# Turning the experts' gather round: one-hot blocks as weights, token rows as the moving operand

## The chip, the cores and the metric

The kernel runs on one core of a Trainium2 chip. The metric is the time of one execution in device microseconds, as the median of several runs; one more execution is taken by the profiler, and its trace is what is read below. Only TensorE (PE), VectorE (DVE), ScalarE (ACT), GpSimd (POOL) and SyncE (SP, which issues the transfers) of that core are in play.

## What is computed

One layer of a decoder over 288 tokens: 256 of one prompt and 8 sequences of 4. A mixer of two linear-attention branches, then a mixture of experts, each under a modulated norm. Everything is fp32. The part that matters here, cut from the reference (M = 288 tokens, D = 1024, 16 experts of hidden width 512, two experts for each token):

```python
def _moe(h, w_gr, b_gr, w_er, b_er, w_g, w_u, w_d):
    ...
    comb = (one_hot(group) * g_w)[:, :, None] * within[:, None, :]   # token x group x expert, two non-zero
    out = jnp.zeros_like(hf)
    for g in range(N_GROUPS):
        a = jnp.einsum('md,edf->mef', hf, w_g[g])
        u = jnp.einsum('md,edf->mef', hf, w_u[g])
        hid = jax.nn.silu(a) * u * comb[:, g, :, None]
        out = out + jnp.einsum('mef,efd->md', hid, w_d[g])
```

The kernel does not compute every expert for every token. It gathers, for each expert, up to 64 of the tokens that chose it, runs the expert on these, and scatters the results back.

## The kernel before, in words

The mixer, the output projection and the router take the first 640 us or so. The router leaves `h2t`, the 288 normed token rows in three tiles of 128, 128 and 32 tokens (`TILES`), each row of 1024 numbers; `rank`, for each token and expert its place among that expert's tokens; and `comb`, its weight.

The 16 experts are then worked off as 8 pairs, `expert_block(i)`, in the order in which they are numbered. A pair has 128 slots (`PAIR`), 64 (`SLOTS`) for each of its two experts. VectorE builds from `rank` the one-hot blocks `Dg` (token x slot, one block for each token tile) and, times `comb`, `Dc`. TensorE's order in a pair is written out by hand, and so is that of the other engines:

- gate: `hg`, the gathered rows turned (1024 features over 8 blocks of 128 partitions, 128 slots), times the gate weights into bank 2; each expert's 64 slots are one product of 64 weight columns and 512 moving columns, two of them side by side (`products`);
- three transposes of `Dc` into bank 4, from which VectorE copies the scatter matrix `DT_`;
- up: the same with the up weights into bank 3;
- `gather(i + 1)`: the next pair's rows, in both turned and gathered form in one step: for each of 8 feature blocks and each of 3 token tiles a product with 128 features of `h2t` as weights and the 128 columns of `Dg` as the moving operand, into banks 0 and 1. VectorE copies bank 0 into the first half of `hg`, ScalarE bank 1 into the second (`gather_read`, L1827 and L2229);
- four transposes of `hid`, the activated hidden rows, into bank 5, and a wait for VectorE's copy of them (L1847);
- down: 16 products into banks 6 and 7, copied by VectorE (L1850) and ScalarE (L2245) into `yt`;
- scatter: 8 products of 288 columns, into banks 4 to 7, which VectorE adds to `acc` (L1854). From the fifth on a product waits until VectorE has added the one that stood in its bank.

A pair's gate waits for both copies of `gather_read`. The first gather, `gather(0)`, stands before the loop; the last pair has none behind it. SyncE issues the transfers: each expert's weights are 3 x 2 MB, loaded for a pair at a time, 4 MB a transfer; gate weights have two buffers, up and down weights one each. The load of a pair's up weights is issued when the pair before has finished its up products, the down weights likewise, and the gate weights when the gate products two pairs before are over. Tokens beyond an expert's first 64 are handled in a loop of `overflow` blocks, which runs no block with these inputs. The norm and the output follow.

All of TensorE's instructions are recorded by two helpers, `mm` (L431) and `tr` (L434), so a line alone doesn't tell one product from another; shapes and the order do. In the records an fp32 product is two loads of weights and two streams; a transpose is one of each.

Of the kernel before, what the change touches and what calls it, by code (L numbers as in the profile page):

```python
# [19 lines left out]
ACT = mybir.ActivationFunctionType  # L20
# [132 lines left out]
def _program(nc, ctx, I, O, known):  # L153
# [130 lines left out]
    EW = carve(3, 2, 4096, at=mixer_only)  # L284
    yrow = carve(3, D, at=mixer_only)
    top[0] = persistent
    h2t = carve(3, D)
# [171 lines left out]
    def named(prefix, names):  # L459
        return {n: ctx.enter_context(nc.semaphore(f"{prefix}_{n}")) for n in names}  # L460


    STEPS = ("one_hot", "dispatch", "scatter_matrix", "scatter_matrix_read", "gathered", "gather_read0",
             "gather_read1", "gate",
             "up", "softplus_step", "softplus", "log_sigmoid", "sigmoid", "silu", "hidden", "turned", "turned_read",
# [22 lines left out]
    def _(pe):  # L488
# [504 lines left out]
        def gather(i, n):  # L993

            pe.wait_ge(n["dispatch"], i + 1)
            for g in range(2):
                for k in range(4):
                    for m, (o, w) in enumerate(TILES):
                        last = mm(pm[g][:, PAIR * k:PAIR * k + PAIR],
                                  h2t[0:w, m, 512 * g + 128 * k:512 * g + 128 * k + 128],  # L1000
                                  Dg[0:w, m].rearrange("p a b -> p (a b)"), m == 0, m == 2)
                last.then_inc(n["gathered"], 1)

        def expert_block(i, n, loaded_sem, second, gates, gates_loaded, more):
# [34 lines left out]
            for g in range(2):  # L1039
                for k in range(4):  # L1040
                    last = products(pm[6 + g], hidT, 2, k, g, 4)
                last.then_inc(n["down"], 1)
            pe.wait_ge(n["down_read0"], i + 1)
            for d in range(KD):
# [8 lines left out]
        def experts():  # L1053
# [6 lines left out]
            pe.wait_ge(*when("read h2t21"))  # L1060
            gather(0, main_sems)
            with pe.Fori(0, TWO_PAIRS) as i:
                expert_block(2 * i, main_sems, expert_loaded, 1, EW[:, 0], (expert_loaded[0], 16 * (i + 1)), True)
                expert_block(2 * i + 1, main_sems, expert_loaded, 1, gate2, (gate2_loaded, 16 * (i + 1)), True)
# [6 lines left out]
            def one_over(j):  # L1071
                gather(j, over_sems)
                expert_block(j, over_sems, over_loaded, 0, EW[:, 0], (over_loaded[0], 16 * (j + 1)), False)

# [21 lines left out]
    def _(dve):  # L1096
# [723 lines left out]
        def dispatch_pair(pair):  # L1820

            two = bass.ds(2 * pair, 2)
            dispatch(rank[:, :, two], comb[:, :, two], main_sems, pair + 1, 2)

        def gather_read(i, n):
            dve.wait_ge(n["gathered"], 2 * i + 1)
            V.tensor_copy(hg[:, 0:4, :], pm[0][:, 0:4 * PAIR].rearrange("p (k s) -> p k s", s=PAIR)) \  # L1827
                .then_inc(n["gather_read0"], 1)

        def expert_block(i, n, next_dispatch):  # L1830
# [13 lines left out]
            if next_dispatch:  # L1844
                gather_read(i + 1, n)
            dve.wait_ge(n["turned"], i + 1)
            V.tensor_copy(hidT, pm[5][:, 0:4 * PAIR].rearrange("p (k s) -> p k s", s=PAIR)) \  # L1847
                .then_inc(n["turned_read"], 1)
            dve.wait_ge(n["down"], 2 * i + 1)
            V.tensor_copy(yt[0:PAIR, 0:512], pm[6][0:PAIR, :]).then_inc(n["down_read0"], 1)  # L1850
            dve.wait_ge(n["added"], KD * i + 1)
            for d in range(KD):
# [3 lines left out]
        def experts():  # L1856
# [20 lines left out]
            step(V.tensor_copy(expB, b[:, 0:OVER]))  # L1877
            step(V.tensor_copy(rankO, mid(b[:, 16:16 + OVER], 3)), "read table", "tables")
            gather_read(0, main_sems)
            with dve.Fori(0, NE // 2 - 1) as i:  # L1880
# [4 lines left out]
            def one_over(j):  # L1885
# [13 lines left out]
                dve.wait_ge(over_sems["picked"], 6 * j + 6)  # L1899
                dispatch(rankJ.unsqueeze(2), combJ.unsqueeze(2), over_sems, j + 1, 1)  # L1900
                gather_read(j, over_sems)
                expert_block(j, over_sems, None)
# [27 lines left out]
    def _(act):  # L1930
# [275 lines left out]
        def router():  # L2206
# [16 lines left out]
            act.wait_ge(*when("ed"))  # L2223
            A.activation(rs_["p1"], rs_["p1"], ACT.Exp).then_inc(mark("router_by_scalar", "eexp"), 1)
            token_major(2)

        def gather_read(i, n):
            act.wait_ge(n["gathered"], 2 * i + 2)
            A.activation(hg[:, 4:8, :], pm[1][:, 0:4 * PAIR].rearrange("p (k s) -> p k s", s=PAIR), ACT.Copy) \  # L2229
                .then_inc(n["gather_read1"], 1)  # L2230

        def expert_block(i, n, more):
# [9 lines left out]
            if more:  # L2242
                gather_read(i + 1, n)
            act.wait_ge(n["down"], 2 * i + 2)
            A.activation(yt[0:PAIR, 512:1024], pm[7][0:PAIR, :], ACT.Copy).then_inc(n["down_read1"], 1)  # L2245

        def experts():
            gather_read(0, main_sems)
            with act.Fori(0, NE // 2 - 1) as i:
                expert_block(i, main_sems, True)  # L2250
            expert_block(NE // 2 - 1, main_sems, False)
            act.wait_ge(*when("tables"))

            def one_over(j):
                gather_read(j, over_sems)
                expert_block(j, over_sems, False)

            overflow(act, one_over)
# [18 lines left out]
    def _(pool):  # L2277
# [48 lines left out]
        def router():  # L2326
# [6 lines left out]
            G.memset(comb, 0.0)  # L2333
            G.memset(rt, 0.0).then_inc(mark("cleared", "rt zero"), 1)

            G.memset(acc, 0.0).then_inc(main_sems["added"], 1)
# [186 lines left out]
```

## Time and profile before

| what | value |
|---|---|
| time, median of 3 runs | 963.03 us (962.93 to 964.56) |
| profiled execution, its own time | 962.34 us |
| span of the profiled execution | 960.4 us |
| TensorE busy | 876.6 us (91%) |
| weight loads (PEld) busy | 594.3 us (62%) |
| VectorE busy | 399.9 us (42%) |
| ScalarE busy | 258.2 us (27%) |
| moved by DMA | 190.65 MB, mean 199 GB/s |
| transfers of expert weights | 24, of 4096 KB each |

A busy TensorE is not one at its peak: products are pipelined, and a record counts as busy while it lasts, also where the weight loads are what sets the pace. The granted clock, beside each stretch in the views by windows, is a share of the full 2.4 GHz: 1.00 is that, 0.50 is 1.2 GHz. The share of the DMA engines is a mean over 16 and can come out a little above 1.

### The profile page before, as it was taken

To read this page: it belongs to the slowest core of one execution; us is meant where nothing else is said; L and a number is where in the kernel's file an instruction comes from. 1 tells how busy PE (TensorE), PEld (TensorE's weight loads), DVE (VectorE), ACT (ScalarE), POOL (GpSimd) and SP (SyncE) were. 2 spreads that over 40 slices of the span, in tenths; PEclk is the share of its full clock that TensorE was granted. 3 is DMA by queue.
4 is the path that set the end of the run, shared out by engine and by line. 5 is a ranking of instruction groups with operands and counts; after the bars stand their busy time and mean duration, and the time that the engine had idled before them with its cause. 6 is when DMAs were issued, how large, how long until landed. Compare 5 with 4: busy or idle time off the path is not lost.

```text
span 960.4 us, 12485 instructions
## 1 busy us (share of the span) xinstructions
PE 876.6 (91%) x4791; PEld 594.3 (62%) x4791; DVE 399.9 (42%) x992; ACT 258.2 (27%) x626; POOL 35.2 (4%) x84
## 2 busy tenths in 40 slices
PE   5889999898898899999999978779999999999995
PEld 3557777666666798879887736555544544544533
DVE  3120004656687855664555384341222222222216
ACT  3121103665554333434335320121011011011012
POOL 0000000000400000000001003000000000000000
PEclk9969999999998999999999957957999999999998
DMA  8947666522557321222216318991999998997621
GB/s 206 347 142 228 205 222 213 177 89 88 172 179 240 113 87 45 88 88 69 65 44 170 108 48 246 326 387 50 349 375 338 347 377 331 354 363 265 254 96 51
DMA packets 134412, 190.65 MB, mean 199 GB/s; under 512 B 6656, under 2 KB 90283, under 8 KB 134309
## 3 DMA queue, kind: packets, MB, share of 16 engines
q1 hardware_dynamic: 134360, 189.94, 58.7%
q8 instruction: 35, 0.57, 0.2%
q14 instruction: 17, 0.14, 0.1%
HBM read 178.98 MB, written 10.95 MB: 198 GB/s over the span
## 4 chain that ended last, share of the span: by engine, by line
PE 80%; DVE 10%; ACT 4%; issue 2%; SPq 2%; DMA 1%; DVEq 0%; POOL 0%; ACTq 0%; POOLq 0%
PE bank L431 78%; PE bank L434 3%; DVE arena L1693 2%; DMA arena<-in_w_ada 1%; DVE arena L1271 1%; DVE arena L1847 1%; DVE arena L1134 1%; ACT arena L1945 1%; SPq L2365 0%; ACT arena L1938 0%; DVE arena L1256 0%; ACT arena L1936 0%; ACT arena L1949 0%; DVE arena L1571 0%; ACT arena L2042 0%
## 5 line engine op out<-in xcount | busy, mean ns | idle before, releaser
L431 PE MATMUL bank<-arena 128*128 128x288 f32 (+8 forms) x4494 | 834.9, 414 | 60.4 <-DVE arena L1158 8.6
L431 PEld LDWEIGHTS bank<-arena 128*128 128x128 f32 (+4 forms) x4494 | 559.0, 174 | 322.2 <-issue 178.2
L434 PE MATMUL bank<-arena 128*128 128x128 f32 (+6 forms) x297 | 50.3, 302 | 18.7 <-DMA arena<-in_w_conv 7.3
L434 PEld LDWEIGHTS bank<-arena 128*128 128x128 f32 (+6 forms) x297 | 35.8, 154 | 38.9 <-issue 19.5
L2042 ACT ACTIVATE arena<-arena 128x288 f32<-128x288 f32 (+1 forms) x56 | 25.1, 448 | 122.0 <-DVE arena L1256 122.0
L1854 DVE TENSOR_TENSOR arena<-arena,bank 128x288 f32<-128x288 f32 x64 | 28.8, 455 | 29.4 <-PE bank L431 28.0
L1271 DVE SCALAR_TENSOR_TENSOR arena<-arena 128x312 f32<-128x312 f32 x72 | 39.4, 547 | 2.5
L1834 DVE SCALAR_TENSOR_TENSOR arena<-bank,arena 128x512 f32<-128x512 f32 x8 | 5.5, 692 | 77.2 <-ACT arena L2239 77.2
L1125 DVE TENSOR_TENSOR arena<-bank,arena 128x18 f32<-128x18 f32 x24 | 4.2, 174 | 77.9 <-PE bank L431 77.9
L2229 ACT ACTIVATE arena<-bank 128x512 f32<-128x512 f32 x8 | 4.8, 598 | 111.7 <-PE bank L431 111.7
L1940 ACT ACTIVATE arena<-arena 128x288 f32<-128x288 f32 (+4 forms) x60 | 33.5, 558 | 2.0
L2075 ACT ACTIVATE arena<-bank 128x288 f32<-128x288 f32 x40 | 16.2, 405 | 53.9 <-PE bank L431 30.2
L1256 DVE SCALAR_TENSOR_TENSOR arena<-arena 128x288 f32<-128x288 f32 (+1 forms) x56 | 25.9, 463 | 8.7 <-ACT arena L1940 8.7
L1434 DVE TENSOR_TENSOR arena<-arena 128x512 f32<-128x512 f32 x28 | 18.9, 690 | 23.0 <-PE bank L431 23.0
L1938 ACT ACTIVATE arena<-arena 128x288 f32<-128x288 f32 (+4 forms) x60 | 28.0, 466 | 1.9
L1504 DVE TENSOR_TENSOR arena<-arena,bank 128x512 f32<-128x512 f32 x24 | 16.5, 689 | 26.6 <-PE bank L431 26.6
L1936 ACT ACTIVATE arena<-arena 128x288 f32<-128x288 f32 (+2 forms) x57 | 25.5, 448 | 4.9 <-DMA arena<-in_cc 4.1
L2235 ACT ACTIVATE arena<-bank 128x512 f32<-128x512 f32 x8 | 4.8, 597 | 81.1 <-PE bank L431 81.1
L2245 ACT ACTIVATE arena<-bank 128x512 f32<-128x512 f32 x8 | 4.8, 598 | 71.0 <-PE bank L431 71.0
L1945 ACT ACTIVATE arena<-bank,arena 128x288 f32<-128x288 f32 x19 | 9.5, 500 | 48.7 <-PE bank L431 48.7
L1850 DVE COPY arena<-bank 128x512 f32<-128x512 f32 x8 | 5.5, 691 | 32.4 <-PE bank L431 32.4
L1827 DVE COPY arena<-bank 128x512 f32<-128x512 f32 x8 | 5.5, 692 | 31.1 <-PE bank L431 31.1
(238 smaller groups left out, 441.4 us busy)
## 6 DMA issues: line engine op xcount, KB each, us to landing
arena<-in_w_in SPq DMA_DIRECT2D x36, 1024.0 KB, 6.8
arena<-in_w_exp_gate SPq DMA_DIRECT2D x8, 4096.0 KB, 13.9
arena<-in_w_exp_up SPq DMA_DIRECT2D x8, 4096.0 KB, 17.1
arena<-in_w_exp_down SPq DMA_DIRECT2D x8, 4096.0 KB, 13.0
arena<-in_w_ada SPq DMA_DIRECT2D x24, 1024.0 KB, 5.6
arena<-in_state_gla SPq DMA_DIRECT2D x4, 1024.0 KB, 6.9
out_gla_s<-arena SPq DMA_DIRECT2D x4, 1024.0 KB, 8.9
arena<-in_w_out SPq DMA_DIRECT2D x4, 1024.0 KB, 6.1
```

The costliest lines, as they stand in the source:

```text
L431: return T.matmul(out, lhsT, rhs, start=start, stop=stop)
L434: return T.transpose(out, in_, ident[0:n, 0:n])
L1256: V.scalar_tensor_tensor(sg, y, 0.0, sg, ALU.min, ALU.subtract) \
L1271: V.scalar_tensor_tensor(y, x[:, j:j + YW], wv(j), y, ALU.mult, ALU.add) \
L1434: V.tensor_tensor(Lm[0:n, hs, 0:n], LT[0:n, hs, 0:n], mid(const(f"level{lv}")[0:n, 0:n], HG), ALU.mult) \
L1693: last = V.scalar_tensor_tensor(st, st, eSs[:, s, h:h + 1], pm[4 + j][:, P * q:P * q + P], ALU.mult, ALU.add)
L1854: V.tensor_tensor(acc[:, d, :], acc[:, d, :], pm[4 + d % 4][:, 0:TOK], ALU.add).then_inc(n["added"], 1)
L1936: A.activation(dst, src, ACT.Abs).then_inc(mark(kind, event + " abs"), 1)
L1938: A.activation(dst, dst, ACT.Exp, scale=-1.0).then_inc(mark(kind, event + " exp"), 1)
L1940: A.activation(dst, dst, ACT.Ln, bias=one[0:n]).then_inc(mark(kind, event), 1)
L1945: A.activation(dst, src, ACT.Ln, bias=const("eps")[0:n], scale=scale) \
L2042: A.activation(sg, sg, ACT.Exp).then_inc(mark("proj_by_scalar", f"sig{s3}"), 1)
```

## The change

The gather makes rows first and turns them afterwards. For each half of the 1024 features there are three products, one for each token tile, with the one-hot block `Dg` (128 tokens x 128 slots) as weights and 512 columns of the token rows `h2t` as the moving operand; they give 128 slots x 512 features in bank 0 or 1. VectorE (bank 0) and ScalarE (bank 1) copy these into a new tile `rows` (`rows_read`, in the places of the old `gather_read`). A new step on TensorE, `turn_rows`, turns `rows` by eight transposes of 128 x 128 back into banks 0 and 1, and `gather_read` copies them into `hg` as before, now after the copies out of the down products. In a pair `turn_rows` for the next one stands between down and scatter; for the first pair it stands right behind `gather(0)`.

The third token tile is used at all of its 128 rows, so it is cleared once by GpSimd, ahead of the memset of `acc`, and ScalarE's copy of the third token tile waits for that. The one-hot block has zeros in the rows that no token fills.

```diff
+    rows = carve(D, at=mixer_only + 3 * 2 * 4096)
...
             for g in range(2):
+                for m in range(3):
+                    last = mm(pm[g][0:PAIR, :], Dg[:, m].rearrange("p a b -> p (a b)"),
+                              h2t[:, m, 512 * g:512 * g + 512], m == 0, m == 2)
+                last.then_inc(n["gathered"], 1)
+
+        def turn_rows(i, n):
+
+            for g in range(2):
+                pe.wait_ge(n[f"rows_read{g}"], i + 1)
                 for k in range(4):
-                    for m, (o, w) in enumerate(TILES):
-                        last = mm(pm[g][:, PAIR * k:PAIR * k + PAIR],
-                                  h2t[0:w, m, 512 * g + 128 * k:512 * g + 128 * k + 128],
-                                  Dg[0:w, m].rearrange("p a b -> p (a b)"), m == 0, m == 2)
-                last.then_inc(n["gathered"], 1)
+                    c = 4 * g + k
+                    last = tr(pm[g][:, PAIR * k:PAIR * k + PAIR], rows[0:PAIR, 128 * c:128 * c + 128], PAIR)
+                last.then_inc(n["rows_turned"], 1)
...
                 last.then_inc(n["down"], 1)
+            if more:
+                turn_rows(i + 1, n)
             pe.wait_ge(n["down_read0"], i + 1)
...
             gather(0, main_sems)
+            turn_rows(0, main_sems)
...
+        def rows_read(i, n):
+            dve.wait_ge(n["gathered"], 2 * i + 1)
+            V.tensor_copy(rows[0:PAIR, 0:512], pm[0][0:PAIR, :]).then_inc(n["rows_read0"], 1)
+
         def gather_read(i, n):
-            dve.wait_ge(n["gathered"], 2 * i + 1)
+            dve.wait_ge(n["rows_turned"], 2 * i + 1)
...
             if next_dispatch:
-                gather_read(i + 1, n)
+                rows_read(i + 1, n)
             dve.wait_ge(n["turned"], i + 1)
...
             V.tensor_copy(yt[0:PAIR, 0:512], pm[6][0:PAIR, :]).then_inc(n["down_read0"], 1)
+            if next_dispatch:
+                gather_read(i + 1, n)
             dve.wait_ge(n["added"], KD * i + 1)
...
+            act.wait_ge(*when("h2t padding"))
             token_major(2)
 
+        def rows_read(i, n):
+            act.wait_ge(n["gathered"], 2 * i + 2)
+            A.activation(rows[0:PAIR, 512:D], pm[1][0:PAIR, :], ACT.Copy).then_inc(n["rows_read1"], 1)
...
             if more:
-                gather_read(i + 1, n)
+                rows_read(i + 1, n)
             act.wait_ge(n["down"], 2 * i + 2)
             A.activation(yt[0:PAIR, 512:1024], pm[7][0:PAIR, :], ACT.Copy).then_inc(n["down_read1"], 1)
+            if more:
+                gather_read(i + 1, n)
...
+            G.memset(h2t[:, 2, :], 0.0).then_inc(mark("cleared", "h2t padding"), 1)
 
             G.memset(acc, 0.0).then_inc(main_sems["added"], 1)
```

## Rows read from the trace of the kernel before

**Rows 1.** The page: the chain that ended last, shares of the span by engine

```profile
PE 80%; DVE 10%; ACT 4%; issue 2%; SPq 2%; DMA 1%; DVEq 0%; POOL 0%; ACTq 0%; POOLq 0%
```

**Rows 2.** The chain in order of time, a period: start us, us, what

```profile
...
720.26 18.20 PE bank L431 x80
...
739.00 15.47 PE bank L431 x80
...
755.94 18.18 PE bank L431 x80
```

**Rows 3.** Windows of one period: stretch, length, busy (count), clock, DMA share, GB/s

```profile
731.35:767.02 35.67, 34.79 (x168) 17.22 (x167) 9.13 (x18) 3.78 (x6) 0.00 (x0) 1.00 0.95 353
```

**Rows 4.** Timeline: start, us, engine, line, operation, count [idle before <-releaser]

```profile
723.95 0.69 DVE L1850 COPY arena<-bank 128x512 f32<-128x512 f32 x1 [3.84 <-PE bank L431]
...
727.27 3.69 PEld L431 LDWEIGHTS bank<-arena 128*128 128x128 f32 x16 [0.81 <-issue]
727.38 0.60 ACT L2245 ACTIVATE arena<-bank 128x512 f32<-128x512 f32 x1 [7.96 <-PE bank L431]
728.13 3.78 DVE L1854 TENSOR_TENSOR arena<-arena,bank 128x288 f32<-128x288 f32 x8 [3.49 <-PE bank L431]
731.35 0.20 PEld L431 LDWEIGHTS bank<-arena 128*64 128x64 f32 x4 [0.39 <-issue]
...
745.96 8.32 PEld L431 LDWEIGHTS bank<-arena 128*128 128x128 f32 x48 [0.81 <-issue]
...
754.40 0.42 PEld L434 LDWEIGHTS bank<-arena 128*128 128x128 f32 x4
754.40 0.66 PE L434 MATMUL bank<-arena 128*128 128x128 f32 x4
```

**Rows 5.** Timeline of weight loads in the mixer, under full-width products of 512 columns

```profile
419.83 0.19 PEld L431 LDWEIGHTS bank<-arena 128*128 128x128 f32 x1 [0.24 <-issue]
420.26 0.19 PEld L431 LDWEIGHTS bank<-arena 128*128 128x128 f32 x1 [0.24 <-issue]
```

**Rows 6.** Timeline of weight loads from the first gather to the first up products

```profile
645.86 0.93 PEld L431 LDWEIGHTS bank<-arena 128*128 128x128 f32 x4 [0.22 <-issue]
...
647.73 0.93 PEld L431 LDWEIGHTS bank<-arena 128*128 128x128 f32 x4 [0.23 <-issue]
...
658.97 0.29 PEld L431 LDWEIGHTS bank<-arena 128*64 128x64 f32 x4 [0.23 <-issue]
...
659.88 0.24 PEld L431 LDWEIGHTS bank<-arena 128*64 128x64 f32 x2 [0.62 <-issue]
...
667.57 0.20 PEld L431 LDWEIGHTS bank<-arena 128*64 128x64 f32 x4
```

**Rows 7.** Where the clock rises: windows (columns of rows 3), timeline, and chain

```profile
656.00:657.00 1.00, 1.00 (x5) 0.65 (x3) 0.00 (x0) 0.00 (x0) 0.00 (x0) 0.50 0.00 0
...
661.00:662.00 1.00, 1.00 (x6) 0.28 (x4) 0.00 (x0) 0.00 (x0) 0.00 (x0) 0.95 0.00 0
...
927.00:928.00 1.00, 1.00 (x4) 0.21 (x2) 0.00 (x0) 0.00 (x0) 0.00 (x0) 0.67 0.00 0
...
930.00:931.00 1.00, 1.00 (x4) 0.28 (x3) 0.00 (x0) 0.00 (x0) 0.00 (x0) 0.63 0.00 0
...
926.80 12.86 PE L431 MATMUL bank<-arena 128*64 128x512 f32 x48 [0.88 <-DVE arena L1847]
...
579.95 38.39 PE bank L431 x144
...
586.00:588.00 2.00, 2.00 (x10) 1.38 (x9) 0.69 (x3) 0.00 (x0) 0.36 (x1) 1.00 0.94 281
```

**Rows 8.** Timeline of GpSimd: the memset of `acc`

```profile
614.79 2.02 POOL L2336 MEMSET arena<- 128x2304 f32 x1
```

**Rows 9.** Issue of one load of up weights, and its landing by the page

```profile
746.21 0.37 SPq L2431 DMA_DIRECT2D arena<-in_w_exp_up  x1
...
arena<-in_w_exp_up SPq DMA_DIRECT2D x8, 4096.0 KB, 17.1
```

More of the change, by code:

```diff
@@ L460, in named @@
         return {n: ctx.enter_context(nc.semaphore(f"{prefix}_{n}")) for n in names}
-    STEPS = ("one_hot", "dispatch", "scatter_matrix", "scatter_matrix_read", "gathered", "gather_read0",
-             "gather_read1", "gate",
+    STEPS = ("one_hot", "dispatch", "scatter_matrix", "scatter_matrix_read", "gathered", "rows_read0", "rows_read1", "rows_turned",
+             "gather_read0", "gather_read1", "gate",
              "up", "softplus_step", "softplus", "log_sigmoid", "sigmoid", "silu", "hidden", "turned", "turned_read",
@@ L1072, in one_over @@
                 gather(j, over_sems)
+                turn_rows(j, over_sems)
                 expert_block(j, over_sems, over_loaded, 0, EW[:, 0], (over_loaded[0], 16 * (j + 1)), False)
@@ L1878, in experts @@
             step(V.tensor_copy(rankO, mid(b[:, 16:16 + OVER], 3)), "read table", "tables")
+            rows_read(0, main_sems)
             gather_read(0, main_sems)
@@ L1900, in one_over @@
                 dispatch(rankJ.unsqueeze(2), combJ.unsqueeze(2), over_sems, j + 1, 1)
+                rows_read(j, over_sems)
                 gather_read(j, over_sems)
@@ L2224, in router @@
             A.activation(rs_["p1"], rs_["p1"], ACT.Exp).then_inc(mark("router_by_scalar", "eexp"), 1)
+            act.wait_ge(*when("h2t padding"))
             token_major(2)
+        def rows_read(i, n):
+            act.wait_ge(n["gathered"], 2 * i + 2)
+            A.activation(rows[0:PAIR, 512:D], pm[1][0:PAIR, :], ACT.Copy).then_inc(n["rows_read1"], 1)
         def gather_read(i, n):
-            act.wait_ge(n["gathered"], 2 * i + 2)
+            act.wait_ge(n["rows_turned"], 2 * i + 2)
             A.activation(hg[:, 4:8, :], pm[1][:, 0:4 * PAIR].rearrange("p (k s) -> p k s", s=PAIR), ACT.Copy) \
@@ L2242, in expert_block @@
             if more:
-                gather_read(i + 1, n)
+                rows_read(i + 1, n)
             act.wait_ge(n["down"], 2 * i + 2)
             A.activation(yt[0:PAIR, 512:1024], pm[7][0:PAIR, :], ACT.Copy).then_inc(n["down_read1"], 1)
+            if more:
+                gather_read(i + 1, n)
         def experts():
+            rows_read(0, main_sems)
             gather_read(0, main_sems)
@@ L2254, in one_over @@
             def one_over(j):
+                rows_read(j, over_sems)
                 gather_read(j, over_sems)
```

## The prediction

> **What bounds the kernel now.** The chain that ended last comes first: four fifths of it is TensorE work, and hardly any is a wait for a transfer [rows 1]. The same chain in order of time shows where the change sits. From 661 to 917 us it repeats with a period of 35.68 us, one period for each pair of experts, and all of it is TensorE but for one VectorE copy (L1847) [rows 2]. So a microsecond taken from TensorE inside this period is a microsecond of the end, as long as nothing else is nearly as long. One thing is: the DMA engines are 0.95 busy in a period, while VectorE and ScalarE are busy for 9.1 and 3.8 of 35.67 us [rows 3]. The timeline of one period then gives the order on TensorE: gate, three transposes, up, gather, four transposes of the hidden rows, a wait, down, scatter [rows 2, 4].
>
> In the gather the weight loads are the bound. 48 loads of 128x128 fill 8.32 us without a gap, 173 ns each [rows 4]; a product of 128 fp32 columns is made of two such load-and-stream records and streams for less than that.
>
> **Gathers 1 to 7, inside the period.** Old: from the first gather load at 745.96 to the first load of the hidden rows' transposes at 754.40, 8.44 us [rows 4]. New: per half of the 1024 columns three products (one per token tile) of a 128x128 one-hot block with 512 token columns, six products, at two records each twelve records. The trace has this very form, full width and 512 columns, at full clock: loads of 0.19 us start every 0.43 us, each hidden by the stream before it [rows 5]. So 0.2 us for the first load and 12 x 0.43 = 5.16 us. The transposes' first load can hide under the last stream, so the saving is 8.44 + 0.1 - 5.36 = 3.2 us, or 3.1 if it doesn't hide; I take 3.15. The third token tile at 128 rows instead of 32 costs columns nothing: the number of streamed columns is what it was (24 x 128 = 6 x 512).
>
> Added on TensorE: eight transposes of 128x128 between down and scatter. The four of the hidden rows load in 0.42 us, 0.105 each, and last 0.66 us with their tail [rows 4]. Eight in a row: 0.84 us if the scatter's loads follow at once, 1.32 if each four pay their tail. The pause on going from the 64-wide to the 128-wide products stands there already, ahead of the scatter's first load at 727.27, and is not paid twice. I take 0.9, near the first, since both semaphores that `turn_rows` waits for are long up: VectorE's copy of half 0 and ScalarE's copy of half 1 follow a gather that ends a whole down product (some 7 us) earlier, and a copy takes 0.6 to 0.7 us [rows 4].
>
> Added beside TensorE: the two copies of the rows, one on VectorE, one on ScalarE, in the places where `gather_read` stood, and `gather_read` itself moved behind the copy out of the down products. Nothing late follows by the rows. VectorE: the down copy is over at 724.64, the first four transposes at about 728.0, `gather_read` 0.69 us, so 728.7; the first scatter product, which came out at 728.13, now comes at about 729.0, so the additions (L1854, 3.78 us for eight) start no later than the product lets them. Queued behind a late copy would be these additions, and TensorE's fifth scatter product waits for the first of them; about 0.3 us of room. ScalarE: the down copy ends at 727.98, the second four transposes at about 728.4, the read at 729.0; the next gate starts at 731.35 + 0.9 [rows 4]. If the cover of 0.3 us is gone, it costs what is over, 0.2 us a period at most.
>
> Net per period 3.15 - 0.9 = 2.25 us, bounds 1.8 (3.1 - 1.3) and 2.4. Seven gathers lie inside a period: **15.8 us**, 12.5 to 16.8.
>
> **Gather 0.** It runs at half clock. Its loads come in groups of six, 1.87 us apart; eight groups back from the first gate load at 658.97 it starts at 644.0 and takes 15.0 us; the first gate and its three transposes take 8.6 us until 667.57 instead of the 7.6 of later periods [rows 2, 4, 6], because the clock goes up only 2.1 us into the gate. All through the gather TensorE counts as busy and the granted clock stays at 0.50 [rows 7]. New: twelve streams of 512 columns with no gap. At half clock one takes 0.86 us (0.24 + 0.62 of the gate's loads [rows 6]). Dense streams had the clock raised 2.1 us after their start at 658.97, 3.9 us after 926.80, about 6.0 us after 579.95 [rows 6, 7]. With the middle one: first stream 644.3, 4.5 records at half clock, 7.5 at 0.43, end 651.4. Then the exposed tail, which the old order hides: ScalarE's copy of half 1 0.85 with its signal (the first four transposes lie beside it), the second four 0.45, gate at 652.7, up at 660.3, 7.3 us earlier. With 2.1 us the gain is 8.2, with 6.0 it is 6.3. I take **7.0**, a little to the late side.
>
> **Edits at nothing.** The memset of the padded tile is 1024 columns on GpSimd; the one of 2304 takes 2.02 us at 614.79 [rows 8], so 0.9 us, ahead of it in the queue. Waiting on it are ScalarE's third token tile, some 15 us later, and, through the `acc` memset behind it, the first scatter matrix near 660: both covered; uncovered it would cost 0.9 once. The last pair has no gather behind it and the end after it is untouched.
>
> **Transfers.** SyncE issues each load when a TensorE product frees its buffer, so a shorter period moves the issues too. The tightest is up: issued at 746.21, 17.1 us to landing [rows 9], needed by the next up at 739.00 + 35.68 = 774.7, 28.5 later; with the new period 26.2 later. Three transfers of 4096 KB need 0.95 x 35.67 = 33.9 us of the engines by share, against a new period of 33.4: at worst they fall back 0.5 us a period, 3.5 in seven, against 9 us of room. So no wait, but little is left.
>
> **Sum.** 15.8 + 7.0 = 22.8 us off the profiled run's 962.34: 939.5. The median of the runs shown, 963.03, is 0.7 above it, so **940.2**.
>
> **Rivals.** (a) The clock does not go up in gather 0: 12 x 0.86 = 10.3, tail 1.7 at half clock, gate at 656.3 and 8.6 us long as before, up at 664.9: gain 2.7 instead of 7.0, time 944.5. For it: the old gather never raised it in 15 us. Against: the gaps of the old one are gone, and the three dense stretches above raised it within 6 us.
>
> (b) The transfers become the bound. If they go no faster than the 353 GB/s of a period [rows 3] however early they are issued, the period stays 35.67; the 9 us of room carry four periods at 2.25 and the last three win nothing: 15.8 - 6.8 + 7.0 = 16.0, time 947. Against: at that mean the engines are 0.95 busy, so 353 is no ceiling yet.
>
> (c) The clock falls in the middle of the period, and the kernel is slower. In the last pair a stretch of waits and four transposes before 926.80 was followed by half clock from about 927.3 to 930.7 [rows 7], 3.4 us in which 1.7 us of streaming is lost. The change adds a second stretch without products to each period, half a microsecond of pause and 0.9 of transposes. One fall a period leaves 0.55 us of the 2.25; from 2.25 / 1.7 = 1.3 falls a period on it is slower. With a fall at both places: 7 x (3.4 - 2.25) = +8.1, gather 0 as in (a), -2.7: 968.4. Against: the stretch there is now, 1.5 us with four transposes and a wait, leaves the clock at 1.00 in all five periods [rows 3].
>
> The Trainium skill, "TensorE: Matmul & The Clock Gate", Part 4: PE-mode transpose, says that the full clock does not engage for transposes, since they are not counted as work in the same way as products. By that rule eight more of them a period speak for (c). The trace of before has transposes at full clock in every period, which bears the rule out only where they stand with long waits.
>
> (d) The transposes don't pipeline, 0.3 us each as single ones: 2.4 a period, gain 0.75 x 7 + 7.0 = 12.3, time 950.7; the 0.42 us for four loads speaks against.
>
> **How the numbers follow.** Forecast 0.74, with its own range 937 to 943.5 (gather 0 at 6.3 to 8.2, the period at 2.0 to 2.4, and about 1.5 us either way for where the clock falls in the last pair); (a) 0.12; (b) 0.06; (c) 0.03; (d) 0.03; no change through something not seen 0.02. The range for 8 in 10 takes in (a) on the high side and the best bounds on the low one: 936.5 to 945.5. Faster than by 0.2% (1.9 us, about what a measurement here can tell from none) in all but (c) and the unseen: 0.95; same 0.02; slower 0.03.
>
> **What would show it.** A period of 33.4 us in the chain; twelve 512-column records 0.43 us apart in the gather; eight transposes in about 0.9 us after down, with the scatter's loads right behind; the granted clock at 1.00 through every period; gather 0 rising within it. It is wrong if an up product waits for its weights, if the scatter waits for additions, or if half clock shows between 670 and 900 us.

## The result

| | before | changed |
|---|---|---|
| median | 962.98 us (4 runs, 961.65 to 964.56) | 936.03 us (4 runs, 930.9 to 938.96) |
| ratio | | 0.9714, 95% interval 0.9668 to 0.976 |
| profiled execution, its own time | 962.34 us | 938.96 us |
| span of the profiled execution | 960.4 us | 937.0 us |
| TensorE busy | 876.6 us (91%) | 853.8 us (91%) |
| period of a pair | 35.67 us | 33.26 us |

The kernel is 2.9% faster. The forecast was 940.2 us with a range of 936.5 to 945.5, so the direction was right and the time lay 0.5 us under the range. The profiled execution came within 0.5 us of the sum made for it (938.96 against 939.5), but by luck: what it had too small (1.1 us in the periods, 0.9 in the first gather, 0.4 ahead of it) and what it did not have (1.8 us behind the last addition) nearly cancel. And a reason that the prediction gave for most of the gain turned out to be wrong.

The chain of the changed kernel in order of time (start us, us, what) is still TensorE but for the copy now at L1863; a period goes from 706.28 to 739.55, where it was 35.68 us [rows 2]:

```profile
706.28 7.09 PE bank L432 x32
713.37 1.02 PE bank L435 x8
714.40 10.92 PE bank L432 x48
725.31 0.55 PE bank L435 x3
725.86 12.38 PE bank L432 x44
...
739.55 5.76 PE bank L432 x25
```

Down is over at 713.37, the eight transposes take 1.02 us in this view with the pause that stood there before, and the scatter follows. The timeline of the same period (start, us, engine, line, operation, count, idle before) answers to [rows 4]:

```profile
699.55 0.30 PEld L432 LDWEIGHTS bank<-arena 128*128 128x128 f32 x2 [0.81 <-issue]
700.09 0.19 PEld L432 LDWEIGHTS bank<-arena 128*128 128x128 f32 x1 [0.24 <-issue]
...
704.38 0.14 PEld L435 LDWEIGHTS bank<-arena 128*128 128x128 f32 x1 [0.24 <-issue]
704.81 0.60 PE L435 MATMUL bank<-arena 128*128 128x128 f32 x4
...
713.30 0.86 PEld L435 LDWEIGHTS bank<-arena 128*128 128x128 f32 x8 [0.81 <-issue]
714.00 0.69 DVE L1843 COPY arena<-bank 128x512 f32<-128x512 f32 x1 [3.33 <-PE bank L435]
714.13 3.70 PEld L432 LDWEIGHTS bank<-arena 128*128 128x128 f32 x16
714.99 3.78 DVE L1872 TENSOR_TENSOR arena<-arena,bank 128x288 f32<-128x288 f32 x8 [0.30 <-PE bank L432]
```

Twelve records 0.43 us apart; the transposes' first load at 704.38 hides under the last of them; eight transposes load in 0.86 us and the scatter's first load comes 0.83 us after theirs. VectorE's read ends 0.3 us before the first addition can start, the room that was forecast. So a period is 3.25 us shorter in the gather and 0.83 us longer behind down: 2.42 us less.

The first gather begins at half clock and sees it rise within (loads, and a window: stretch, length, busy counts, granted clock, DMA share, GB/s):

```profile
646.30 0.27 PEld L432 LDWEIGHTS bank<-arena 128*128 128x128 f32 x1 [0.52 <-issue]
646.81 0.19 PEld L432 LDWEIGHTS bank<-arena 128*128 128x128 f32 x1 [0.24 <-issue]
...
651.10 0.42 PEld L435 LDWEIGHTS bank<-arena 128*128 128x128 f32 x4 [0.49 <-ACT arena L2250]
651.68 0.20 PEld L432 LDWEIGHTS bank<-arena 128*64 128x64 f32 x4 [0.16 <-DVE arena L1843]
...
646.00:647.00 1.00, 1.00 (x3) 0.46 (x2) 0.00 (x0) 0.00 (x0) 0.00 (x0) 0.77 0.79 291
```

The second four transposes wait 0.49 us for ScalarE's copy, the exposed tail. The first gate loads at 651.68, at 658.97 before [rows 6].

Where 23.4 us of span went, stretch by stretch, before minus changed: 0.4 ahead of the first gather (643.03 and 642.63 us); 7.9 in the first gather, gate and up; 16.9 in seven periods; -1.8 behind the last addition, where 20.3 us became 22.0.

### The profile page after: what moved, and what is told of

It is laid out like the page before. It is cut to its first block, busy times and chain, and to the rows that moved or that the text cites. A ratio compares the mean times of both kernels' runs of the same rounds, so it can differ in the third digit from the quotient of the medians.

```text
span 937.0 us, 12055 instructions
## 1 busy us (share of the span) xinstructions
PE 853.8 (91%) x4567; PEld 564.2 (60%) x4567; DVE 405.6 (43%) x1000; ACT 262.9 (28%) x634; POOL 36.1 (4%) x85
## 4 chain that ended last, share of the span: by engine, by line
PE 80%; DVE 10%; ACT 4%; issue 2%; SPq 2%; DMA 1%; DVEq 0%; POOL 0%; ACTq 0%; POOLq 0%
PE bank L432 76%; PE bank L435 4%; DVE arena L1705 2%; DMA arena<-in_w_ada 1%; DVE arena L1283 1%; DVE arena L1863 1%; DVE arena L1146 1%; ACT arena L1965 1%; SPq L2395 1%; ACT arena L1958 0%; DVE arena L1268 0%; ACT arena L1956 0%; ACT arena L1969 0%; DVE arena L1583 0%; ACT arena L2062 0%
## 5 line engine op out<-in xcount | busy, mean ns | idle before, releaser
L432 PE MATMUL bank<-arena 128*128 128x288 f32 (+10 forms) x4206 | 803.8, 425 | 60.2 <-DVE arena L1170 8.6
L432 PEld LDWEIGHTS bank<-arena 128*128 128x128 f32 (+3 forms) x4206 | 519.6, 172 | 319.7 <-issue 189.5
L435 PE MATMUL bank<-arena 128*128 128x128 f32 (+5 forms) x361 | 61.1, 306 | 18.6 <-DMA arena<-in_w_conv 7.6
L435 PEld LDWEIGHTS bank<-arena 128*128 128x128 f32 (+5 forms) x361 | 45.3, 156 | 48.3 <-issue 29.7
L1866 DVE COPY arena<-bank 128x512 f32<-128x512 f32 x8 | 5.5, 692 | 32.4 <-PE bank L432 32.4
L1997 ACT ACTIVATE arena<-arena 128x288 f32<-128x288 f32 x8 | 3.5, 443 | 50.8 <-DVE arena L1741 50.8
```

Source lines behind the costliest of these rows:

```text
L432: return T.matmul(out, lhsT, rhs, start=start, stop=stop)
L435: return T.transpose(out, in_, ident[0:n, 0:n])
```

## The experiments

Each is given as its edit, the expectation on record, and what came out. The ratio is to runs of the kernel before on the same chip, since its median moved between 957.8 and 963.0 from chip to chip. Lines cut from a diff or a view are marked by three dots.

**1. The same kernel again.** No edit.

> The changed kernel as it is, to see where one execution differs from another. First theory (the clock outside the pairs): the runs shown lie 8 us apart although the work is the same; the stretch from the first gather to the last addition stays within 1 us of the 271.9 us that the first profile of it shows (642.63 to 914.50), and what differs is the stretch behind it (22.5 us there, 20.8 in the kernel before) and the stages before the gather. Median 934 to 938. Rival (the transfers): the pairs themselves differ, periods go from 33.26 to 33.8 us or more in some, and the stretch from first gather to last addition moves by 3 us or more.

935.41 us, ratio 0.9732 (0.9707 to 0.9758). The profiled execution, 935.32 us, is the median one, and the periods are the same to 0.02 us. The stretch from the table product just ahead of the first gather to the last addition is 270.9 us, 1.5 less than in the first profile, and what is behind it takes 20.0 us instead of 22.0. Both differences are the clock. Windows of the first profile, then of this one, in the last pair's down products and in the last transposes:

```profile
903.00:904.00 1.00, 1.00 (x4) 0.30 (x2) 0.00 (x0) 0.00 (x0) 0.00 (x0) 0.50 0.00 0
929.00:930.00 1.00, 1.00 (x7) 0.79 (x5) 0.35 (x1) 0.60 (x1) 0.00 (x0) 0.50 0.00 0
```

```profile
903.00:904.00 1.00, 1.00 (x8) 0.39 (x6) 0.00 (x0) 0.00 (x0) 0.00 (x0) 1.00 0.00 0
926.00:927.00 1.00, 0.87 (x8) 0.55 (x6) 1.00 (x3) 0.53 (x1) 0.00 (x0) 1.00 0.06 16
```

The first theory holds, though with 1.5 us where it gave 1, the last pair's clock; the transfers are out. The kernel before, run 17 times beside it, lay between 956.49 and 964.71: it spreads as much, which three runs did not show.

**2 and 3. The first gather alone, and the others alone.** `gather_old` is the gather of the kernel before.

```diff
             if more:
-                gather(i + 1, n)
+                gather_old(i + 1, n)
...
-            if more:
-                turn_rows(i + 1, n)
```

> Only the first gather is turned round, gathers 1 to 7 are the old ones. By the profiles the first gather and gate end 7.9 us earlier (667.57 - 0.4 against 659.26), so 963 - 7.9 = 955, 953.5 to 957; period 35.7 us as before. Rival: the first gather's gain is an accident of where the clock rose in that one execution: then 958 to 961 and a gate at half clock.

```diff
-            gather(0, main_sems)
-            turn_rows(0, main_sems)
+            gather_old(0, main_sems)
```

> The first gather is the old one, gathers 1 to 7 are turned round. Seven periods of 33.26 instead of 35.68 us: 963 - 16.9 = 946, 944.5 to 948, and the first gather at half clock with 15 us. Together with the run that turns the first gather alone it should add up to the whole, 24 to 25 us. Rival: the two parts share something (the transfers' start, the clock) and don't add up by more than 2 us.

954.82 us and 944.70 us, ratios 0.9919 and 0.9841: 7.1 and 17.2 us, which add up to 24.3 where the whole has 26.5 (23.3 to 28.2 by its interval). The 2.2 us between them are more than the expectation left to its theory and lie within the interval. The traces show no sharing: in the first run the up products of pair 0 end 24.3 us after the first table product, 24.2 in the whole change; in the second the periods are 33.26 us. The first holds a surprise: two of its seven periods, with the old gather, are 37.4 us instead of 35.67. A window in one of them:

```profile
784.00:785.00 1.00, 1.00 (x4) 0.29 (x2) 0.00 (x0) 0.00 (x0) 0.00 (x0) 0.50 1.06 393
```

After the wait for the hidden copy the clock fell for some 3.4 us, 1.7 us lost: the fall that rival (c) feared from the change, in a period with the old gather.

**4. Each transpose twice.** In a pair `turns` is 2.

```diff
-                for k in range(4):
+                for k in [0, 1, 2, 3] * (turns):
```

> Each of the eight transposes inside the periods is done twice, to price them in place. By the load's pace, 0.105 us each: 0.86 us a period, 33.26 to 34.1, seven periods 6.0 us, 942 to 943 where the changed kernel has 936 to 937. Rival (the clock counts transposes as rest): with 1.9 us of transposes on end the granted clock falls behind them, half clock shows in the scatter, and a period grows by 2.5 us or more, 953 or slower.

942.46 us, ratio 0.9812; period 34.13 us, 0.87 more. Loads of the sixteen, and the period as a window, clock 1.00:

```profile
712.02 1.73 PEld L435 LDWEIGHTS bank<-arena 128*128 128x128 f32 x16 [0.81 <-issue]
...
698.52:732.64 34.12, 33.24 (x148) 14.68 (x148) 9.81 (x19) 4.37 (x7) 0.00 (x0) 1.00 0.98 370
```

The price is 0.108 us for a transpose in a chain, and the clock does not fall behind 1.7 us of them. Rival (c), and with it the Trainium skill's statement in "TensorE: Matmul & The Clock Gate", Part 4, that transposes don't count as products do, costs nothing here.

**5. The transposes right behind the gather.** `turn_rows(i + 1, n)` moves from behind down to behind `gather(i + 1, n)`, and the reads of the turned rows with it.

> The transposes of the rows stand right behind the gather instead of behind down, so that TensorE meets ScalarE's copy of the second half of the rows (about 0.85 us with its signal) with no work in between, and then four transposes more (0.45). Behind down 0.83 us go away. First theory (the place behind down is cover): +1.30 - 0.83 = +0.47 us a period, 33.26 to 33.7, seven periods 3.3 us, 938 to 939.5 beside 935.4 of the changed kernel. Rival (the place is worth nothing): 935 to 936.5.

938.58 us, ratio 0.9741; period 33.77, 0.51 more. TensorE stands 0.49 us for ScalarE's copy in each pair. So the place behind down is cover, and worth what was worked out.

**6, 7 and 8. Dense streams in TensorE's waits.** Products on constants, `dense(count)`, stand ahead of the router's products, its third token tile, the rank products and the table; in the last run also in the last pair's waits and around the last norm.

```diff
+        def dense(count):
+            n = len(ring_names)
+            pe.wait_ge(*when(f"read {ring_names[n - 4]}"))
+            for c in range(count):
+                mm(pm[n % 4][:, 0:512], ident, cst[:, 0:512])
```

> The old gather everywhere, with products of 512 columns on constants, their results unread, filling TensorE's waits from the end of the output projection to the first gather, so that the clock is up when the gather starts. Theory (nearly all that the change wins in the first gather is the clock): the first gather goes from 15.0 to 8.4 us, its gate loses 1.0, and the router's own products about 2 us: 962 - 9.5 = 952.5, 951 to 955. Rival (the columns, not the clock): the clock falls again in the old gather, or its pace does not depend on it; 960 to 964.

> The changed kernel with the same filling before the first gather. Only three of its twelve records ran at half clock, 1.3 us; with the router's 2 us: 935.4 - 3.5 = 932, 930.5 to 934. Beside the same filling in the kernel before, the change then wins 16.9 us in seven periods and about 1.8 in the first gather (8.4 against 5.4 and a tail of 1.3), 18.7 in place of 26.5. Rival: the first gather's gain has nothing to do with the clock, and the two differ by 24 us or more as without the filling.

> The changed kernel with the filling before the first gather and also in the two waits of the last pair, before the last norm's products and before the last transposes, where the profiles show half clock for 3 to 9 us, at other places from execution to execution. Theory (the clock makes the spread and the late end): last pair up to 1.7, norm 1.4, transposes up to 2 us less: 927 to 930, the runs within 4 us of each other. Rival (the spread comes from the transfers or the stages before): the median falls by the router's share alone, 932, and the runs still lie 6 us or more apart.

960.07, 934.74 and 935.64 us, ratios 0.9987, 0.972 and 0.9725: next to nothing, and all three expectations missed. The filling held the clock up through the router, but the rank and table products that follow it are sparse and the clock fell about when they ran (at 640.2 us in 6), so the old first gather ran at 0.50 as ever. So 6 and 7 did not try what they were meant to try (12 does). In 8 the spread of 3.3 us was small, but the stretch behind the last addition took 24.0 us. TensorE stands 4.42 us there ahead of the norm's products, for nothing that the chain names, where it stands 3.49 in the changed kernel; why is not shown, nor that filling the waits there would pay.

**12. Dense streams right ahead of the old first gather.**

```diff
             pe.wait_ge(*when("read h2t21"))
+            dense(6)
             gather(0, main_sems)
```

> The kernel before with six products of 512 columns on constants right ahead of the first gather, their results unread: 6.5 to 8.5 us of work more, which has the clock up when the old gather starts. Theory (the old first gather is long for its half clock alone): the gather takes 8.4 instead of 15.0 us and its gate 7.6 instead of 8.6, so the time stays within 2 us of 962. Rival (the old gather lets the clock fall, or costs as much at full clock): 967 to 971.

960.29 us, ratio 0.9984. The clock is up at 645.5, and the old gather then takes about 8.3 us at full clock, not 15.0, and holds it (the first row has the gate's first loads with the gather's 48):

```profile
649.07 8.53 PEld L431 LDWEIGHTS bank<-arena 128*128 128x128 f32 x51 [0.24 <-issue]
...
652.00:654.00 2.00, 2.00 (x13) 1.52 (x13) 0.64 (x1) 0.00 (x0) 0.00 (x0) 1.00 0.00 0
```

So of the first gather's 15.0 us, 6.7 were the half clock; the old gather does not raise the clock but keeps it once it is up.

**10 and 11. Fewer columns a product.** The changed kernel, its gather in products of 128 and of 256 columns.

```diff
-                for m in range(3):
-                    last = mm(pm[g][0:PAIR, :], Dg[:, m].rearrange("p a b -> p (a b)"),
-                              h2t[:, m, 512 * g:512 * g + 512], m == 0, m == 2)
+                for k in range(4):
+                    for m in range(3):
+                        last = mm(pm[g][0:PAIR, 128 * k:128 * k + 128], Dg[:, m].rearrange("p a b -> p (a b)"),
+                                  h2t[:, m, 512 * g + 128 * k:512 * g + 128 * k + 128], m == 0, m == 2)
```

> As the changed kernel, one-hot blocks as weights, but each product of the gather with 128 token columns instead of 512, so 24 products and 48 weight loads as before the change. Theory (the gather's pace is that of its weight loads): 48 x 0.173 = 8.3 us, period 33.26 + 3.15 = 36.4, and with the first gather at half clock again 11 to 14 us of it: 935.4 + 22 + 5 = 962, 958 to 966, that is, the whole gain gone. Rival (it is the operands' roles that win, rows read along instead of across): 935 to 940.

> As the changed kernel, with 256 token columns a product, 12 products and 24 weight loads. Theory (loads of 0.173 to 0.19 us hide under a stream of 0.213): 24 x 0.215 = 5.16 us as with 512 columns, period 33.3, 935 to 936.5. Rival (a load costs something beside the stream, so fewer loads are better all the way): period 34 to 34.9, 940 to 946.

935.32 and 936.78 us, ratios 0.9738 and 0.9744; periods 33.47 and 33.29 us. With 256 columns the period is the one expected, the time 0.3 us above its range. With 128 columns the theory falls flat: as many products and loads as the old gather, and nearly the whole gain stays. Its 48 loads:

```profile
695.16 5.43 PEld L432 LDWEIGHTS bank<-arena 128*128 128x128 f32 x48 [0.81 <-issue]
```

113 ns each, where the same number took 8.32 us [rows 4]. Records of 512, 256 and 128 columns follow one another after 0.43, 0.215 and 0.113 us, in proportion to the columns, which speaks for loads that hide even here. The pace of the old gather was not that of weight loads. The trace of the kernel before could have told: in the mixer, right behind the loads of [rows 5], thirty loads of full width under products of 128 columns go in 3.43 us, 114 ns each:

```profile
420.69 3.43 PEld L431 LDWEIGHTS bank<-arena 128*128 128x128 f32 x30 [0.24 <-issue]
```

And the row of [rows 4] that seemed to have no gap has them: a row of the timeline joins records that lie close together. The same stretch as a window (busy time of TensorE, then of its loads), first in the kernel before:

```profile
745.96:754.28 8.32, 8.32 (x50) 6.50 (x48) 1.38 (x2) 0.00 (x0) 0.00 (x0) 1.00 1.03 386
```

The loads are busy for 6.50 of 8.32 us. In the first gather, at half clock, the same pauses stand open in the timeline, 0.22 to 0.23 us ahead of each change to the third token tile's 32 rows and back:

```profile
645.14 0.50 PEld L431 LDWEIGHTS bank<-arena 32*128 32x128 f32 x2 [0.23 <-issue]
645.86 0.93 PEld L431 LDWEIGHTS bank<-arena 128*128 128x128 f32 x4 [0.22 <-issue]
```

New theory: the change from 128-row products to the third token tile's 32-row products, and back, costs a pause. The old gather makes 16 of them (two for each of eight feature blocks, the last on the way to the transposes behind it), the changed one none, since it uses the third tile at 128 rows.

**13, 14 and 15. Only the padding; all but the padding; half the changes.** In 13 the memset and the wait for it come with the edit, as in the change.

```diff
                     for m, (o, w) in enumerate(TILES):
                         last = mm(pm[g][:, PAIR * k:PAIR * k + PAIR],
-                                  h2t[0:w, m, 512 * g + 128 * k:512 * g + 128 * k + 128],
-                                  Dg[0:w, m].rearrange("p a b -> p (a b)"), m == 0, m == 2)
+                                  h2t[:, m, 512 * g + 128 * k:512 * g + 128 * k + 128],
+                                  Dg[:, m].rearrange("p a b -> p (a b)"), m == 0, m == 2)
```

> The gather of the kernel before, token rows as weights and 128 columns of the one-hot block, no transposes of rows; only the third token tile is used at 128 rows, cleared once, instead of 32. New theory (the change from 128-row to 32-row products and back costs a pause, and full-width loads alone go every 0.113 us as in the run with 128 columns): gather 48 x 0.113 = 5.45, period 35.67 - 2.9 = 32.8, and a first gather that raises the clock: 962 - 20 - 7.5 = 934.5, 931.5 to 937. Rival (the roles of the operands: rows of tokens as weights load slower than one-hot blocks): period 35.5 to 35.7, 958 to 962.

```diff
+                    w = TILES[m][1]
-                    last = mm(pm[g][0:PAIR, :], Dg[:, m].rearrange("p a b -> p (a b)"),
-                              h2t[:, m, 512 * g:512 * g + 512], m == 0, m == 2)
+                    last = mm(pm[g][0:PAIR, :], Dg[0:w, m].rearrange("p a b -> p (a b)"),
+                              h2t[0:w, m, 512 * g:512 * g + 512], m == 0, m == 2)
```

> The changed kernel with the third token tile at its 32 rows, so that each gather changes between 128-row and 32-row products four times instead of never. Theory (each such change costs about 2.9 / 16 = 0.18 us, more under long streams): +0.5 to 0.8 us a period, 33.8 to 34.1, 939 to 942. Rival (padding is worth nothing under 512 columns): 33.26 and 935 to 936.5.

```diff
-                    for m, (o, w) in enumerate(TILES):
+                    turn = (2, 0, 1) if k % 2 else (0, 1, 2)
+                    for m in turn:
...
```

> The kernel before with its three token tiles in the order 0, 1, 2 and then 2, 0, 1 for the next block of features, so that two 32-row products stand side by side and a gather changes between 128 and 32 rows 8 times instead of 16. Theory (the changes are the cost): half of 2.9 us less, period 34.2, seven periods 10 us, 949 to 953. Rival (the 32-row products are slow by themselves, however they stand, or the cost lies elsewhere): period 35.6, 960 to 962.

929.09, 940.72 and 945.25 us, ratios 0.9680 (0.9649 to 0.971), 0.9808 and 0.9849. Gather loads with 0 changes, then with 8, of the two kernels with 48 products' records:

```profile
699.00 5.43 PEld L431 LDWEIGHTS bank<-arena 128*128 128x128 f32 x48 [0.81 <-issue]
```

```profile
705.30 6.97 PEld L431 LDWEIGHTS bank<-arena 128*128 128x128 f32 x48 [0.81 <-issue]
```

As windows, the first with 0 and the second with 8 changes:

```profile
699.00:704.43 5.43, 5.43 (x50) 5.43 (x49) 1.39 (x2) 0.00 (x0) 0.00 (x0) 1.00 1.04 388
```

```profile
705.30:712.27 6.97, 6.97 (x50) 6.00 (x49) 1.38 (x2) 0.00 (x0) 0.00 (x0) 1.00 1.04 388
```

The loads of the old gather stand still for 1.82 us, 0.12 at each of the 15 changes inside it; with 8 changes it is 0.97, again 0.12 each, and with none nothing. In time, 5.43, 6.97 and 8.32 us: (6.97 - 5.43) / 8 = 0.19 and (8.32 - 5.43) / 15 = 0.19 us a change. TensorE counts as busy through all of it. In the changed kernel without its padding the four changes stand open as gaps of 0.76 us before a load that elsewhere waits 0.24 and hides:

```profile
702.50 0.29 PEld L432 LDWEIGHTS bank<-arena 32*128 32x128 f32 x2 [0.76 <-issue]
703.55 0.30 PEld L432 LDWEIGHTS bank<-arena 128*128 128x128 f32 x2 [0.76 <-issue]
```

Its period is 33.99, 0.73 more: 0.18 a change again. The next weights are not loaded under the running stream when the number of rows differs. The Trainium skill, "TensorEngine Tiling (Array Packing)", Tiling Modes, Key Properties, says that changing the tiling mode, not just the tile, drains the engine. The pauses agree with it if a 32-row product counts as another mode, which no trace here names.

The times follow from the periods and the first gather, to within 0.8 us. In 13, 28.7 us beside the kernel before on this chip: 7 x 3.03 = 21.2 in the periods and 7.8 up to the first up products. In 15, 12.6 us: 10.4 in the periods (34.18 us) and 1.4 up to the first up products; the first gather, with half the changes, takes 12.9 us at half clock instead of 15.0. Both medians lie below the ranges expected for them, since those started from 962, and the kernel before took 957.8 on this chip.

The padded kernel of before has a period of 32.64 us, 3.03 less than 35.67 and 0.62 less than the changed kernel. By the period, padding alone gives more than the whole change; turning the gather round, with eight transposes and two more copies a pair, costs 0.6 us a period of it. By the time the two ratios, 0.9680 and 0.9732 (1), have intervals that just touch.

The clock in the first gather goes with the changes too. Windows at about 650 us, with 0 and with 8 changes:

```profile
649.00:650.00 1.00, 1.00 (x10) 1.00 (x10) 0.69 (x1) 0.00 (x0) 0.00 (x0) 0.90 0.00 0
```

```profile
649.00:650.00 1.00, 1.00 (x5) 0.78 (x5) 0.36 (x1) 0.00 (x0) 0.00 (x0) 0.50 0.00 0
```

With none or four (14) it rises inside the gather; with 8 or 16 it stays at half up to the gate, unless it is up before (12).

**9. The transposes in the wait for the hidden copy.** Pointed to by 4 and 5: TensorE rests 0.88 us in each pair for VectorE's copy, and the transposes need 0.83.

```diff
             last.then_inc(n["turned"], 1)
+            if more:
+                turn_rows(i + 1, n)
             pe.wait_ge(loaded_sem[2], 16 * (i + 1))
...
-            if more:
-                turn_rows(i + 1, n)
             pe.wait_ge(n["down_read0"], i + 1)
```

> The eight transposes of the rows stand in TensorE's wait for VectorE's copy of the turned hidden rows (0.88 us of rest in each period) instead of behind down; the reads of them follow that copy. By the first theory (TensorE is still the bound): the second half of the rows is copied 0.85 us after the gather, so transposes fill the wait and down starts when it does now: 33.26 - 0.83 = 32.43 us a period, seven periods 5.8 us, 935.4 - 5.8 = 929.6, 928 to 931.5. Rival (the transfers are now the bound, since the engines are already 1.01 busy and move 379 GB/s in a period of 33.26): 32.43 us would need 388 GB/s; then periods grow back to 33 us or more from the third or fourth on, an up or down product waits for its weights, 932.5 to 935.4.

926.67 us, ratio 0.9636 (0.9606 to 0.9666); period 32.43, to the hundredth. In the chain twelve transposes stand in one piece and the wait is gone; as a window, TensorE is busy all of the period and the transfers keep up at 1.03 and 386 GB/s:

```profile
703.26 1.35 PE bank L435 x12
704.61 18.17 PE bank L432 x80
...
698.09:730.52 32.43, 32.43 (x140) 13.84 (x140) 9.73 (x19) 4.38 (x7) 0.00 (x0) 1.00 1.03 386
```

So rival (b) does not bite even here, and this version is faster than both kernels. The time fell by more than the period: 8.7 us from the 935.41 of the changed kernel, where seven periods give 5.8, and 1.3 us below the range. That is not explained; the profiled execution, 930.67, lies 4.0 above the median.

**16 and 17. The last 32-row transpose.** The third of the three transposes ahead of up, at 128 rows, in versions 9 and 13.

```diff
-                last = tr(pm[4][0:PAIR, o:o + w], Dc[0:w, m].rearrange("p a b -> p (a b)"), w)
+                last = tr(pm[4][0:PAIR, o:o + P], Dc[:, m].rearrange("p a b -> p (a b)"), P)
```

> The transposes of the rows in TensorE's wait (as in the run that put them there, period 32.43 us), and in addition the third of the three transposes of the weighted one-hot block at 128 rows instead of 32, so that no product or transpose of a period changes the number of rows. Theory (0.18 us for a change of rows, also among transposes, and the up products behind change columns anyway): one to two changes fewer, 32.07 to 32.25 us a period, 1.4 to 2.9 us in eight pairs, ratio to the kernel before 0.961 to 0.963. Rival (no pause among transposes, and 128 columns in place of 32 cost 0.04 to 0.1 us): 32.43 to 32.55.

> The gather of the kernel before with the padded third token tile (period 32.64 us) and the same third transpose at 128 rows. Theory: 32.3 to 32.45 us a period, ratio to the kernel before 0.9655 to 0.967. Rival: 32.64 to 32.75.

927.28 and 929.72 us, ratios 0.9666 (0.9632 to 0.97) and 0.9672; periods 32.37 and 32.56, 0.06 to 0.08 less. Both lie between the theory and the rival, a little nearer the rival: 32 rows less among the transposes, paid for with 128 columns instead of 32 and with 64-wide products behind that change anyway, win a third of the 0.19 us of one change in a stream of products, and nothing that the time shows.

## Why the prediction missed, step by step

**What bounds the kernel.** Right: TensorE, one period a pair. A change of the period came out about sevenfold in the time: 17.2 us for 16.9 (3), 7.1 for 6.1 (4), 3.2 for 3.6 (5); only 9, 8.7 for 5.8, stands apart.

**"In the gather the weight loads are the bound."** Wrong. It was read from a row of loads that seemed to have no gap [rows 4]; the row joins them over fifteen pauses of 0.12 us, and without these the loads go at 113 ns (10, 13). The 173 ns are that pace and the pauses together. What failed is the step that set the third tile's padding at nothing: "costs columns nothing: the number of streamed columns is what it was". The columns do stay; but the padding takes away 16 changes of row count at 0.19 us, and alone shortens the period by 3.03 us (13), where the gather of the whole change lost 3.25. The sum came out near all the same, because the 512-column form was priced from its own row [rows 5], which is right whatever had slowed the old one.

**The terms of the period.** 3.15 forecast, 3.25 measured; transposes 0.9 forecast, 0.83 measured, both at the good end of their bounds. Net 2.42 against 2.25, at the good end of 2.4: 16.9 us instead of 15.8. The cover (5), the price of a transpose (4), the copies beside TensorE and the transfers (9) were as worked out.

**Gather 0.** 7.0 forecast, 7.9 and 7.7 measured in the two profiles of the changed kernel. The clock rose 2.9 and 3.4 us after the gather's first load (at 646.5 and 646.9 us), between the early row, 2.1, and the one taken, 3.9. That was an early draw: in four more profiles with the same code up to there (2, 4, 5, 9) it rose 3.5 to 5.8 us after, and the gain was 6.5 to 7.6, so 7.0 was well chosen. That it is the clock was right (12); why the old gather never raised it was not known: with its changes of rows taken away, and nothing else, it does (13).

**From the profile to the median.** "The median of the runs shown, 963.03, is 0.7 above it, so 940.2": this step carried the offset of one execution over to another, and it is the step that failed by most. In the changed kernel the offset measured is -2.9 instead of 0.7: its profiled execution is the slowest of its four. That is 3.6 of the 4.2 us between 940.2 and 936.03. The allowance of 1.5 us for the clock in the last pair left out the other places outside the periods: over the profiles the stretch ahead of the first gather takes 637.1 to 643.5 us in the kernels without filling, and the one behind the last addition 20.0 to 24.4, the same work each time. The half clock in the last pair, which cost both first profiles 1.7 us, stands in 4 of 19 profiles.

**The rivals.** (a) fell: the clock rose in every gather without changes or with four. (b) and (d) fell (9, 4). (c) fell for the change; the falls it feared are in the old periods: 6 of 28 periods in the four profiles with the unaltered old gather in the pairs (the kernel before, 2, 6, 12) took 1.7 us more, none of 98 in fourteen profiles with 0 to 4 changes. Whether the change wins from that on average, beside the terms of the sum, was not measured.

## What to carry to other kernels

A row of records without gaps does not say what sets their pace, and it can hide short pauses: compare its length with the busy time of the same stretch as a window, and look for the same shape elsewhere in the trace at a better pace, before calling it the bound. Keep products of one row count together on TensorE, or pad the odd tile to 128 rows: here that was worth 3 us in a period of 36, more than turning the gather round gives. And a forecast of a median needs the spread of executions on both sides, not one profile's offset.

## What was not expected of the hardware

A change between 128-row and 32-row products costs 0.18 to 0.19 us at full clock, in short streams and long ones (14, 15). The clock can fall to half in a loop that mostly holds it: in the old periods it did so in 6 of 28, right behind a stretch of 1.5 us with four transposes and a wait, 1.7 us each time. The same stretch behind the changed gather never lost it; that the gather's pauses are the reason is not shown. Eight or sixteen transposes in a row did not bring it down.
